# First block of a two-block model on one core: the order of its two attentions, with the linear bias added by VectorE in PSUM

## The reference, cut to what matters

```
h = rms_norm(x); proj = h @ w_in[l]            # 3328 columns
A: 6 query heads, 2 key/value heads of 64: rms_norm of q and k, rotary turn,
   softmax(q k^T / 8) v                          -> mix columns 0 to 383
B: 4 heads, two sets of q and k of 48, v of 96: rms_norm of q and k,
   s = q k^T * 48**-0.5 - slope * |i - j|        (the bias, "alibi")
   p = softmax(s1) - lam * softmax(s2); o = p v; rms_norm(o) -> columns 384 to 767
C: gated linear scan over tokens, both directions; rms_norm, times silu(gate)
                                                 -> columns 768 to 1023
x = x + mix @ w_out[l]
then: x = x + (gelu(conv(gate)) * val) @ w_down[l]
```

## Time and profile before

| | us |
|---|---|
| three runs, median (lowest, highest) | 2944.22 (2942.88, 2944.81) |
| the profiled execution's own time | 2944.41 |
| its span, first to last instruction | 2942.6 |
| mean granted TensorE clock, share of full | 0.961 |

### The profile page before, as it was taken

The page is one execution under the profiler, slowest core; times in us unless marked ns, Lnnn a source line. Parts: engine busy times, 40 slices in busy tenths (PEclk is TensorE's granted clock), DMA queues, the critical chain, the costliest instruction groups (busy, mean ns, idle before and its releaser), DMA issues. The chain is left out here.

```text
span 2942.6 us, 57193 instructions
## 1 busy us (share of the span) xinstructions
PE 2712.1 (92%) x17384; PEld 2423.4 (82%) x17384; DVE 2088.4 (71%) x4674; ACT 1481.8 (50%) x2884; POOL 220.9 (8%) x168
## 2 busy tenths in 40 slices
PE   7989989989985899899999999976999899999997
PEld 6759988679874899899988888855999899988886
DVE  5757767567667658977767777676569777777776
ACT  5545555545432445456655555524454466555554
POOL 0000000000020034400000000200144100000000
PEclk9999999999985999999999999977999999999999
DMA  5225553246540557655567777612577555577775
GB/s 190 85 65 172 184 191 101 72 131 184 184 166 1 162 179 229 188 159 174 174 204 233 232 232 233 206 57 79 154 229 215 158 173 176 171 233 234 234 233 180
DMA packets 194020, 504.57 MB, mean 171 GB/s; under 512 B 22528, under 2 KB 88320, under 8 KB 192512
## 3 DMA queue, kind: packets, MB, share of 16 engines
q1 hardware_dynamic: 193920, 503.33, 55.2%
HBM read 468.64 MB, written 34.60 MB: 171 GB/s over the span
## 5 line engine op out<-in xcount | busy, mean ns | idle before, releaser
L182 DVE TENSOR_TENSOR w_lo<-w_raw,w_hi 128x512 fp32r<-128x512 f32 (+2 forms) x1432 | 973.3, 684 | 341.8 <-ACT w_hi L173 321.4
L173 ACT ACTIVATE w_hi<-w_raw 128x512 fp32r<-128x512 f32 (+2 forms) x1592 | 927.1, 621 | 267.4 <-PE banks_right L217 136.8
L215 PE MATMUL up_up<-hT_hi,w_hi 128*128 128x256 f32 x2048 | 594.4, 290 | 26.8 <-DVE w_lo L182 20.7
L217 PE MATMUL up_up<-hT_hi,w_lo 128*128 128x256 f32 x2048 | 581.6, 284 | 0.0
L216 PE MATMUL up_up<-hT_lo,w_hi 128*128 128x256 f32 x2048 | 581.1, 284 | 0.0
L215 PEld LDWEIGHTS up_up<-hT_hi,w_hi 128*128 128x128 f32 x2048 | 394.8, 193 | 31.2 <-DVE w_lo L182 24.0
L227 PE MATMUL banks_left<-w_hi,expert_hi 128*128 128x512 f32 x1024 | 407.6, 398 | 7.8 <-DVE w_lo L182 7.8
L228 PE MATMUL banks_left<-w_lo,expert_hi 128*128 128x512 f32 x1024 | 406.9, 397 | 0.0
L229 PE MATMUL banks_left<-w_hi,expert_lo 128*128 128x512 f32 x1024 | 406.9, 397 | 0.0
L216 PEld LDWEIGHTS up_up<-hT_lo,w_hi 128*128 128x128 f32 x2048 | 394.4, 193 | 0.0
L217 PEld LDWEIGHTS up_up<-hT_hi,w_lo 128*128 128x128 f32 x2048 | 393.7, 192 | 0.0
(11 more groups left out here) (366 smaller groups left out, 4162.3 us busy)
## 6 DMA issues: line engine op xcount, KB each, us to landing
w_raw<-in_peer_u_c SPq DMA_DIRECT2D x256, 512.0 KB, 3.6
w_raw<-in_peer_v SPq DMA_DIRECT2D x256, 512.0 KB, 3.6
w_raw<-in_w_up_c SPq DMA_DIRECT2D x88, 512.0 KB, 3.7
expert_gelu_held<-expert_gelu SPq DMA_DIRECT2D x256, 128.0 KB, 1.8
expert_back<-expert_gelu_held SPq DMA_DIRECT2D x256, 128.0 KB, 3.4
w_raw<-in_w_down SPq DMA_DIRECT2D x44, 512.0 KB, 4.3
w_raw<-in_w_in_r SPq DMA_DIRECT2D x40, 512.0 KB, 3.6
w_raw<-in_w_in_c SPq DMA_DIRECT2D x32, 512.0 KB, 3.7
```

The costliest lines, as they stand in the source:

```text
L173: self.nc.scalar.activation(self.w_hi[:, k % SLOTS, 0:width], self.raw_half(k, width), ACT.Copy).then_inc(self.sem("w_hi_done"), 1)
L182: self.nc.vector.tensor_tensor(self.w_lo[:, k % SLOTS, 0:width], self.raw_half(k, width), self.w_hi[:, k % SLOTS, 0:width].bitcast(F32), A ...
L215: self.nc.tensor.matmul(bank, hi, self.hT_hi[:, c, :], start=(c == 0), stop=False)
L217: last = self.nc.tensor.matmul(bank, lo, self.hT_hi[:, c, :], start=False, stop=(c == DC - 1))
```

## The change

The row blocks are reordered, so that A's queries and keys come in the first block and C's values and gate in the second. A's norm and rotary turn move to moments 20 to 31, between the levels of the scan. C's output is normed at 40 to 43, B's rows at 44 to 48. B's heads are turned at 49 to 52 and B's eight attention steps come first, at 53 to 64, with the four output halves of chunks 6 and 7 beside the first of them and ten pauses behind. A's heads are turned at 61 to 64, A's six steps follow at 63 to 73; there step g covers both token halves in turn for a pair of heads, so that each pair finishes one chunk of the mix. The output order is 6, 7, 3, 4, 5, 0, 1, 2; twelve of the sixteen output halves (moments 68 to 79) stand beside or behind A's steps. The bias matmuls are gone: in `biggest`, VectorE computes scores * scale + bias in place in PSUM (scalar_tensor_tensor, 128x512) before it takes the maximum, and the table of biases is no longer multiplied by sqrt(48) on the host. ScalarE's root for B's output norm comes between A's exps of steps 2 and 3.

```diff
-    PAUSES = {52: 4, 62: 3}
+    PAUSES = {52: 2, 56: 10}
-    OUT_ORDER = (6, 7, 0, 1, 2, 3, 4, 5)
-    TURN_A, ATT_A, TURN_B, ATT_B = 0, 4, 10, 18
-    MIX_JOB = {6: 6, 7: 6, 0: 7, 1: 7, 2: 8, 3: 17, 4: 17, 5: 18}
+    OUT_ORDER = (6, 7, 3, 4, 5, 0, 1, 2)
+    TURN_B, ATT_B, TURN_A, ATT_A = 0, 8, 16, 20
+    MIX_JOB = {6: 0, 7: 0, 3: 12, 4: 12, 5: 13, 0: 17, 1: 18, 2: 19}
+    TURN_JOB = (1, 2, 3, 4, 5, 6, 7, 8, 9, 10, 11, 14, 15, 16)
...
         for j in range(8):
-            yield 52 + j // 2
+            yield 49 + j // 2
             if j == 0:
                 pe.wait_ge(S["heads_ready"], 2)
             turn_heads_job(self.TURN_B + j, ...)
+            if j == 4:
+                mix_job(0, (6, 7), (S["mixed"], 1))
         for s in range(8 + 4):
-            yield 56 + s
+            yield 53 + s
             if s == 0:
                 pe.wait_ge(S["s_out"], self.ATT_B)
             if s < 8:
                 b_scores(s)
+            else:
+                j = s - 8
+                turn_heads_job(self.TURN_A + j, ...)
             if 2 <= s < 10:
-                turn(6 + s - 2, 9 + s - 2, 1)
+                turn(s - 2)
             if s >= 4:
                 b_values(s - 4)
+        for s in range(6 + 4):
+            yield 63 + s
+            if s == 0:
+                pe.wait_ge(S["s_out"], self.ATT_A)
+            if s < 6:
+                a_scores(s)
+            if s == 5:
+                mix_job(13, (5,), (S["mixed"], 3))
+            if 2 <= s < 8:
+                turn(8 + s - 2)
+            if s >= 4:
+                a_values(s - 4)
+            if s == 4:
+                mix_job(12, (3, 4), (S["mixed"], 3))
+            if s == 8:
+                mix_job(17, (0,), (S["o_free"], 4))
+        mix_job(18, (1,), (S["o_free"], 5))
+        yield 74
+        mix_job(19, (2,), (S["o_free"], 6))
... ScalarE
-        yield 20
-        act.wait_ge(self.row_free, 2)
-        A.activation(self.sg[:], self.rows[:, :, 256:512], ACT.Silu).then_inc(S["silu_g"], 1)
+        yield 21
+        root(0, A_HEADS + A_KV, 1)
...
+        yield 36
+        act.wait_ge(self.row_free, 4)
+        A.activation(self.sg[:], self.rows[:, :, C_V0 + 256:C_V0 + 512], ACT.Silu)...
+        yield 42
+        root(2, C_HEADS, 2)
+        yield 47
+        root(1, 4 * B_HEADS, 3)
...
+        for s in range(6 + 2):
+            yield 64 + s
+            if s < 6:
+                exps(8 + s, self.ATT_A + s, A_DIM ** -0.5)
+            if s == 2:
+                root(3, B_HEADS, 4)
+            if s == 5:
+                mix_hi(13, (5,))
+            if 2 <= s < 8:
+                turned(8 + s - 2)
+            if s == 4:
+                mix_hi(12, (3, 4))
... VectorE
+        def biggest(g, job, scale, bias):
+            dve.wait_ge(S["s_in"], job + 1)
+            s = self.s_bank(job)
+            if bias is not None:
+                link(V.scalar_tensor_tensor(s, s, scale, bcast_mid(bias, 2), ALU.mult, ALU.add))
+            link(V.tensor_reduce(self.top[:, g, :], s, AX.X, ALU.max))
+            V.tensor_scalar(self.low[:, g, :], self.top[:, g, :], -scale if bias is None else -1.0, None,
+                            ALU.mult).then_inc(S["max"], 1)
...
+        for s in range(6 + 4):
+            yield 63 + s
+            if s < 6:
+                biggest(8 + s, self.ATT_A + s, A_DIM ** -0.5, None)
+            if 1 <= s < 7:
+                dve.wait_ge(S["s_out"], self.ATT_A + s)
+                mark(V.reciprocal(self.rec[:, 7 + s, :], self.sums[:, 7 + s, :]))
+            if s == 2:
+                b_out(1)
+                mean(3, B_HEADS, B_V)
+            if s == 3:
+                inverse(3, B_HEADS, 4)
+                for t in range(TT):
+                    scaled(self.ob, mix_b, 3, t, B_HEADS).then_inc(S["mixed"], 1)
+            if s == 4:
+                mix_lo((3, 4), 2)
+            if s == 5:
+                mix_lo((5,), 4)
+                settle()
+                a_out(0)
```

More of the change, by code:

```diff
@@ L1315, in turn_heads_job, with scores @@
             ins.then_inc(S["s_in"], 1)
-        def scores(job, q, k, bias):
+        def scores(job, q, k):
             pe.wait_ge(S["s_out"], job - 1)
@@ L1339, in turn, with values @@
             ins.then_inc(S["t_in"], 1)
-        def values(g, job, epoch, first, parts):
-            pe.wait_ge(S["t_out"], job + 1)
+        def values(g, epoch, first, parts):
+            pe.wait_ge(S["t_out"], self.TURN_JOB[g] + 1)
             if first:
@@ L1465, in scalar_steps @@
                 A.activation(e, dots, ACT.Exp).then_inc(S["exp_lam"], 1)
[L1466 to L1471, removed]
+        yield 36
+        act.wait_ge(self.row_free, 4)
+        A.activation(self.sg[:], self.rows[:, :, C_V0 + 256:C_V0 + 512], ACT.Silu).then_inc(S["silu_g"], 1)
         yield 39
@@ L1515, in mix_hi @@
                     A.activation(K.hT_hi[:, c, :], src[:, i, :], ACT.Copy, scale=gain).then_inc(S["hi"], 1)
[L1517 to L1529, removed]
         act.wait_ge(S["prod"], 1 + len(self.LV))
         for j in range(8):
-            yield 52 + j // 2
+            yield 49 + j // 2
             heads(self.TURN_B + j, self.bT[:, 2 * j:2 * j + 2, :], B_DIM, self.qk_gain[0:B_DIM, j // 4:j // 4 + 1])
[L1534 to L1539, removed]
-            if s < 8:
[L1541 to L1547, removed]
+        yield 52
+        act.wait_ge(self.out_gains, 1)
+        mix_hi(0, (6, 7))
+        for s in range(8 + 4):
+            yield 54 + s
+            if s < 8:
+                exps(s, self.ATT_B + s, 1.0)
+            else:
+                heads(self.TURN_A + s - 8, self.aT[:, 2 * (s - 8):2 * (s - 8) + 2, :], A_DIM, None)
+            if 2 <= s < 10:
+                turned(s - 2)
+        for s in range(6 + 2):
[10 more added lines that the diff above has]
+                mix_hi(12, (3, 4))
+        yield 72
+        mix_hi(17, (0,))
+        yield 73
+        mix_hi(18, (1,))
+        yield 75
+        mix_hi(19, (2,))
     def mix_gain(self, c):
@@ L1702, in vector_steps @@
         place(0)
+        yield 20
+        next(norm)
+        yield 21
+        next(norm)
         yield 22
@@ L1712, in vector_steps @@
         for i in range(2, len(self.LV)):
+            yield 19 + 2 * i
+            next(norm, None)
             yield 20 + 2 * i
@@ L1715, in vector_steps @@
             place(i)
-            if i >= 5:
-                yield 21 + 2 * i
-                next(norm)
+        for _ in norm:
+            pass
         dve.wait_ge(S["exp_lam"], 1)
@@ L1723, in vector_steps @@
         place(len(self.LV))
[L1724 to L1744, removed]
@@ L1772, in vector_steps @@
[L1772 to L1777, removed]
-                mark(V.reciprocal(self.rec[:, s - 1, :], self.sums[:, s - 1, :]))
-            if s == 0:
-                dve.wait_ge(S["o_free"], 1)
-            next(norm, None)
-        for _ in norm:
-            pass
-        dve.wait_ge(S["s_out"], self.ATT_A + 6)
-        link(V.reciprocal(self.rec[:, 5, :], self.sums[:, 5, :]))
@@ L1786, in vector_steps @@
-        a_out(0)
-        yield 50
-        inverse(2, C_HEADS, 3)
+        yield 40
+        dve.wait_ge(S["o_free"], 1)
+        for t in range(TT):
+            ins = squares(self.oc, mix_c, t)
+        link(ins)
+        for t in range(TT):
+            ins = add_up(2, mix_c, t, C_HEADS)
+        link(ins)
+        mean(2, C_HEADS, C_DIM)
+        yield 43
+        inverse(2, C_HEADS, 2)
         for t in range(TT):
@@ L1793, in vector_steps @@
         V.tensor_tensor(mix_c, mix_c, self.sg[:], ALU.mult).then_inc(S["mixed"], 1)
-        yield 51
-        inverse(1, n_b, 2)
+        dve.wait_ge(self.row_free, 8)
+        for t in range(TT):
+            yield 44 + t
+            mark(squares(b_rows, self.bqk, t))
+        settle()
+        for t in range(TT):
+            yield 45 + t
+            mark(add_up(1, self.bqk, t, n_b))
+        settle()
+        mean(1, n_b, B_DIM)
+        yield 48
+        inverse(1, n_b, 3)
         for t in range(TT):
```

192 lines of the change are left out of this document (79 added, 113 removed).

## The result

The changed kernel takes 2973.51 us (median of 4 runs, 2972.85 to 2978.01) against 2944.51 before. The ratio is 1.0100, its 95% interval 1.0088 to 1.0112. So it is 29 us slower, where I had said 12.6 slower and a range up to 2968: the sign was right, the size was not, and the time lies above the range. The profiled execution of the changed kernel is its slowest run (2978.01, span 2976.2), 4.5 us over the median.

The account below looks back on a forecast made before the run. The prediction took TensorE, busy 92% of the span, as the bound where other engines wait for it. It added 7.0 us at full clock and 6.0 for slow clock to 2944.41, giving 2957, range 2945 to 2968.

Parts of the forecast that it names:

- both parts of the change, clock up: First block's mixing part, reorder and bias move at full clock: 3.5 us a layer slower, +7.0 in all.
- clock of TensorE at 1.2 GHz: A's new stretch, at about half clock: 3.0 us a layer, +6.0 in all.
- the prediction's checkpoints: Layer 0 times: scan product 69.9, B's first scores 137.2, A's first scores 166.8, last half's end 211.7.
- The idle of TensorE ahead of B's heads: During B's norm on VectorE: TensorE idles 5.3 us, where before it idled little.
- the operation at 0.70: VectorE's bias operation in B's steps: 0.80 us with its link, making VectorE's step 2.45 us.
- the 16 us from A's first scores to the first half of chunk 3: A's steps: scores start at 166.8, the half at 182.75, with TensorE idle some 7 us between.
- the loads in the scan and in the entry: ScalarE table loads of 1.28 us: one ahead of the scan's exps, one uncovered in the next entry.
- the slow clock of the old end: End of B's attention in the kernel before: slow clock, put at 2 us a layer, goes with the change.
- I take 3.0 a layer: Clock term for A's new stretch: 3.0 us a layer, between bounds of nothing and 5.4 us.
- a slow chain from 175 to 193: Upper bound of the clock term: the whole chain there at 1.2 GHz adds 5.4 us.
- my second rival: Clock falls in B's steps too, TensorE slower than VectorE: 8 us a layer, 2973; chance 0.10.
- my first rival: Clock stays up in A's stretch because the gaps are short: 2951.4; chance 0.15.

Follow-up runs that it names:

- run 3: The changed kernel with matmuls of zeros filling TensorE's waits from B's norm to A's last turn (also called the filled run): 2951.49 us, ratio to before 1.0020.
- run 5: The changed kernel with A's root moved behind the scan's first exps and the next entry's root table loaded early: 2971.02 us.
- run 1: The kernel before, in its old order, with only B's bias moved to VectorE: 2930.67 us, ratio 0.9957.
- run 6: The kernel before with B's bias on VectorE and 25 matmuls of zeros a layer at the end of B's attention: 2923.51 us, ratio 0.9929.
- the two filled kernels: Run 3 (new order, 2951.49 us) and run 6 (old order, 2923.51 us), both with B's bias on VectorE and matmuls of zeros in TensorE's waits.
- run 2: The changed kernel with B's bias put back as matmuls on TensorE, so the new order alone: 2979.57 us, ratio 1.0120.
- run 4: The changed kernel with matmuls of zeros in A's stretch only, none in B's norm, heads and steps: 2962.54 us, ratio 1.0054.

## Why the prediction was right and wrong

| us, both layers | forecast | measured |
|---|---|---|
| both parts of the change, clock up | +7.0 | +7.0 (run 3) |
| clock of TensorE at 1.2 GHz | +6.0 | +22.0 (run 3 against the changed kernel) |
| in all | +13.0, given as 2957 | +29.0 |

**Right: the times of the steps.** Each of the prediction's checkpoints, from the scan's product to the last half, is met within 1 us, in the changed kernel up to B's first scores and in the filled run behind them. The idle of TensorE ahead of B's heads (4.4 us between 119.5 and 129, where I had 5.3), the operation at 0.70 with VectorE's step at 2.38, the 16 us from A's first scores to the first half of chunk 3, the loads in the scan and in the entry (1.27 each, run 5): all are in the traces.

**Right, but made up of larger parts than a reader of the sum would think.** Over both layers the +7.0 is -13.9 for the bias (run 1), -7.2 for the slow clock of the old end, which goes (run 6), and +28.0 for the order (runs 3 and 6). That these three add up to the whole is no further proof: each is the difference of two neighbours in one chain (before, run 1, run 6, run 3). The forecast had the slow clock of the old end at 2 us a layer, and filled it gives back 3.6. Where the order's 28 us go, the groups of the two filled kernels show, by line:

```profile
L1390 PE MATMUL banks_right<-fill_zero,ident 128*128 128x128 f32 x296 | 41.1, 280 | 0.0
```

```profile
L1387 PE MATMUL banks_right<-fill_zero,ident 128*128 128x128 f32 x100 | 12.2, 276 | 0.0
```

The fillers take 28.9 us more in the new order, while all other work of TensorE is about the same (2727.2 less 41.1 and 2695.4 less 12.2 us busy). So the price of the order is TensorE waiting.

**Wrong: the clock term, "I take 3.0 a layer".** It measured 11.0. I had bounded it by a slow chain from 175 to 193, 5.4 us (its three terms make only 5.05), and that bound was the error: it took for granted that the fall is confined to the stretch in which TensorE is half idle. The traces show it on both sides of that. It comes in B's steps, where VectorE sets a pace of 2.38 us and TensorE is busy 3.75 of 5 us: from 155 on its step is 3.4 us (155.07 to 158.46), now the slower engine, so that more than half of the saving of the bias is gone (6.1 us of it are left between run 2 and the changed kernel, of 13.6). B's part loses 5.0 us. Of these, 1.6 come from the first fall, up to 152.05 (15.84 us from B's first scores, against 14.29 in the filled run), and 3.4 from the second. And it goes on behind A's stretch: output halves and values run at 1.2 GHz into the window 200 to 205 (0.71), 3.1 us more. In A's stretch itself it is 4.1, inside my bounds. Layer 1 of the profiled execution loses more still: from B's first scores to the entry 94.7 us (548.81 to 643.47) against 91.0 in layer 0, where the filled run takes 78.8 in either layer. That makes 28 us for both layers, more than the 22.0 between the medians, and this execution lies above its median. So the traces tell where the time goes, and the medians how much it is.

This was my second rival, to which I gave 0.10 and the very time that came, 2973. Its reason was the earlier trace rows: a window with TensorE busy 3.04 of 4 us that ends at half clock. In the sum I used that row for A's stretch and not for B's steps, whose forecast of 1.9 us of work in 2.45 is the same share. The agreement of the rival's number is partly luck: it put 8 us a layer into B's steps alone, and runs 3 and 4 put about half of the 22 there and half into A's stretch and what follows it.

**The Trainium skill on this.** The largest gap of TensorE among B's steps ahead of the fall at 155 is 1.13 us, and the clock was at 0.50 for the next 10 us. In A's stretch the largest is 2.40, shorter than the 3.57 of the old end that my first rival went by. The Trainium skill's page "TensorE: Matmul & The Clock Gate" has two accounts: in "HAM oscillation — how this bites in real kernels" a long wait for data brings the clock down, in "A second HAM failure mode: psum-queue depth-cycling" frequent short idles between groups of matmuls do. The trace agrees with the second. On the table loads, my prediction weighed the Trainium skill's page "ScalarE: Activation LUTs", section "What ACT_TABLE_LOAD costs", with 2.66 us a switch; the rows after say 1.28 again (176.82 to 178.10, and the root starts at 178.11).

**Still open.** What sets where the first fall comes. In the changed kernel it is at 135 to 140, after two windows of 2.91 and 2.72 us busy out of 5; in runs 4 and 5, the same program for TensorE in that stretch, it is at 125 to 135. Nor can it be read off one row: in the kernel before, windows with TensorE busy 3.81 (145 to 150) and 3.63 of 5 us (185 to 190) are at 1.00.

## What to carry to other kernels

- Where a change puts another engine in charge of a stretch and leaves TensorE with waits between its steps, work the stretch out at 1.2 GHz as well, up to the next dense part; if TensorE's slow step is longer than the other engine's, the slow one is the time.
- Matmuls of zeros into a bank that nobody reads at that moment cost nothing that these traces show where TensorE waits anyway (B's heads to B's first scores take 7.23 us with them and 7.22 without), and bought 22 us here and 7 in the old order. Taking work off TensorE pays less where the clock then falls (6.1 us for 13.6 here), so price the removed work and the clock apart.
- Two edits in one change are best timed one by one: here the useful half (-14 us) was hidden under an order that costs 28 at full clock.

## What the runs showed of the hardware

- The clock did not rise for a while although TensorE was busy without a gap: from 155.07 to 162.80 in the changed kernel, with 0.51 in the window 155 to 160 and 0.50 in the next. In the window 165 to 170, again busy 5.00 of 5 us, it did rise (0.62).
- A multiply and add over 512 elements in place in PSUM took 0.70 us, as long as the maximum over the same elements (0.69). I had put it at 0.75 to 0.80.
- Of two table loads on ScalarE between A's exponentials, 2.56 us, only 0.5 was on the path with the clock up: without them ScalarE stood 0.88 us at the same place for VectorE's means.
